# Strassen's scheme for six more output tiles of the first MLP, and two moves of single steps, in a one-core transformer kernel

## The reference, cut to what matters

```python
def _sq_relu_mlp(h, w1, w2):                     # first block, d_ff = 4096
    return jnp.square(jax.nn.relu(h @ w1)) @ w2
...
        y_x = _sq_relu_mlp(_modulate(x, g_pre_mlp[l], sh2, sc2), w_mlp_in[l], w_mlp_out[l])
        x = x + gt2 * _rmsnorm(y_x, g_post_mlp[l])
...
def mem_group(q_raw, mem_h, w_mem_kv, q_norm, k_norm):       # second block
    k = rmsnorm(kv[:, :, 0], k_norm)             # over the 128 features of each of 4 heads
...
        x = x + (mix @ w_out[l]).astype(x.dtype) # mix: latent attention, recurrence, memory attention
```

## Time and profile before

| | us |
|---|---|
| median of 3 runs | 1296.88 (1296.52 to 1297.44) |
| profiled execution | 1297.27 |
| its span from first to last instruction | 1296.0 |
| TensorE busy | 1281.8 (99%) |
| VectorE, ScalarE, GpSimd busy | 965.0, 781.6, 822.3 |
| granted TensorE clock | 1.0 in the whole span |

### The profile page before, as it was taken

One profiled execution on the slowest core, in us unless ns is written; L12 is line 12 of the kernel. 1 busy time (PEld: TensorE's weight loads), 2 busy tenths in 40 slices (PEclk: granted clock), 3 DMA queues, 4 the chain that ended last, 5 costly groups with the idle time before them and its releaser, 6 DMA issues.

```text
span 1296.0 us, 22880 instructions
## 1 busy us (share of the span) xinstructions
PE 1281.8 (99%) x8718; PEld 1138.4 (88%) x8718; DVE 965.0 (74%) x1685; ACT 781.6 (60%) x1488; POOL 822.3 (63%) x592
## 2 busy tenths in 40 slices
PE   9999999999999999999999999999999999999998
PEld 6787778879999999988788788777789999999998
DVE  5796694878778989834468575747579887987888
ACT  4532585478677585865655547735487655765664
POOL 2643434978778687656467372643378876887785
PEclk9999999999999999999999999999999999999999
DMA  9685235352333333533332112110223332333233
GB/s 378 237 322 205 84 135 208 110 186 93 124 106 100 101 103 107 179 98 101 127 112 82 44 57 74 57 66 33 66 82 103 110 99 98 103 110 115 98 104 109
DMA packets 42125, 156.35 MB, mean 121 GB/s; under 512 B 4384, under 2 KB 5152, under 8 KB 40992
## 3 DMA queue, kind: packets, MB, share of 16 engines
q1 hardware_dynamic: 41136, 151.60, 34.0%
q0 software_dynamic: 448, 2.62, 0.6%
q10 hardware_dynamic: 432, 0.67, 0.1%
HBM read 149.90 MB, written 4.19 MB: 119 GB/s over the span
## 4 chain that ended last, share of the span: by engine, by line
PE 77%; DVE 11%; ACT 5%; POOL 5%; issue 2%; DVEq 0%; ACTq 0%; POOLq 0%
PE bank L879 21%; PE bank L881 20%; PE bank L880 20%; PE bank L1437 2%; POOL wL L3794 2%; PE bank L928 1%; PE bank L930 1%; PE bank L929 1%; PE bank L982 1%; POOL acc L3804 1%; DVE small L2932 1%; POOL wL L3799 1%; PE bank L975 1%; PE bank L942 1%; PE bank L967 1%
## 5 line engine op out<-in xcount | busy, mean ns | idle before, releaser
L3794 POOL TENSOR_TENSOR wL<-raw,wH 128x1024 fp32r<-128x1024 f32 (+1 forms) x91 | 226.1, 2489 | 228.7 <-ACT wH L1805 225.6
L879 PE MATMUL bank<-hH,wH 128*128 128x512 f32 (+1 forms) x544 | 210.4, 387 | 1.6 <-POOL wL L3794 0.6
L881 PE MATMUL bank<-hH,wL 128*128 128x512 f32 (+1 forms) x544 | 200.6, 369 | 0.0
L880 PE MATMUL bank<-hL,wH 128*128 128x512 f32 (+1 forms) x544 | 200.4, 368 | 0.0
L3799 POOL TENSOR_TENSOR wL<-raw,wH 128x512 fp32r<-128x512 f32 (+1 forms) x120 | 154.6, 1289 | 31.1 <-ACT wH L1814 30.5
L879 PE MATMUL bank<-gH,wH 128*128 128x256 f32 x512 | 145.4, 284 | 0.3 <-POOL gL L3799 0.3
L881 PE MATMUL bank<-gH,wL 128*128 128x256 f32 x512 | 144.9, 283 | 0.0
L880 PE MATMUL bank<-gL,wH 128*128 128x256 f32 x512 | 144.9, 283 | 0.0
L1805 ACT ACTIVATE wH<-raw 128x1024 fp32r<-128x1024 f32 (+1 forms) x91 | 95.2, 1048 | 54.6 <-PE bank L881 28.3
L879 PEld LDWEIGHTS bank<-hH,wH 128*128 128x128 f32 x544 | 102.8, 189 | 25.3 <-issue 6.5
L881 PEld LDWEIGHTS bank<-hH,wL 128*128 128x128 f32 x544 | 102.6, 189 | 18.0
(11 more groups left out here) (537 smaller groups left out, 4087.4 us busy)
## 6 DMA issues: line engine op xcount, KB each, us to landing
raw<-in_wall SPq DMA_DIRECT2D x211, 512.0 KB, 3.3
rows<-in_wall SPq DMA_DIRECT2D x24, 1024.0 KB, 11.1
bra<-in_rpbw SPq DMA_DIRECT2D x8, 360.0 KB, 4.5
xq<-in_xt SPq DMA_DIRECT2D x2, 1024.0 KB, 6.9
xT<-in_xn SPq DMA_DIRECT2D x1, 2048.0 KB, 7.6
out_x<-xT SPq DMA_DIRECT2D x1, 2048.0 KB, 8.6
xT<-out_x SPq DMA_DIRECT2D x1, 2048.0 KB, 9.4
out_x<-xT SPq DMA_DIRECT2D x6, 256.0 KB, 2.6
```

Source lines behind the costliest of these rows:

```text
L879: matmul(o, a_h, b_h, start=first, stop=False)
L880: matmul(o, a_h, b_l, start=False, stop=False)
L881: return matmul(o, a_l, b_h, start=False, stop=last)
L3794: tt(wL[i % NHL][:, 0:n], raw[load(c) % NRAW][:, 0:n], wH[i % NHL][:, 0:n].bitcast(F32), ALU.subtract).then_inc(s.w_lo, 1)
```

## The change

Three edits.

1. **Six of the last eight output tiles by Strassen.** `FIRST_MLP` gets three more outer pairs (12, 13, 14; G grows from 26 to 29 pairs), for the output tiles 0 to 5 of the last quarter. Tiles 6 and 7 stay direct, in halves. The forms of the last four activation pairs are now made like all others, bH and bL are gone, and the late half of the tokens for tiles 6 and 7 gets buffers of its own (xlast, xlH, xlL). The residual x is read back into another buffer (xr). The four statistics move into the last pairs: mk0 after product 5 of pair 13, mk1 and mk2 after products 2 and 5 of pair 14, mk3 after the first half of tile 6. Squares and sums of y are regrouped around the last pair.
2. **The first pair's last piece.** `piece_high(0, 6)` and its `piece_rest` go ahead of the steps for the second activation form.
3. **Latent attention.** The pieces of w_out_2 before the items 2, 4, ..., 14 are cut in two: two k-tiles before the item, two behind it.

```diff
@@ plan and pairs
-        if quarter < 3:
-            for j in range(4):
-                for i, odd in ((0, 0), (1, 0), (1, 1), (0, 1)):
-                    tile("w_mlp_out", 2 * j + i, range(8 * quarter + odd, 8 * quarter + 8, 2))
-        else:
-            group([("w_mlp_out", m) for m in range(2)], OUT_ORDER)
-            for m in range(2, 8):
-                tile("w_mlp_out", m, OUT_ORDER)
+        for j in range(4 if quarter < 3 else 3):
+            for i, odd in ((0, 0), (1, 0), (1, 1), (0, 1)):
+                tile("w_mlp_out", 2 * j + i, range(8 * quarter + odd, 8 * quarter + 8, 2))
+    for m in (6, 7):
+        tile("w_mlp_out", m, OUT_ORDER)
...
-             + [("outer", 4 * quarter + j) for j in range(4 if quarter < 3 else 0)]]
+             + [("outer", 4 * quarter + j) for j in range(4 if quarter < 3 else 3)]]
@@ TensorE
+        KEY_PLACE = {(G - 2, 5): 0, (G - 1, 2): 1, (G - 1, 5): 2}
+
+        def memory_statistic(i):
+            statistic_of_halves(f"mk{i}", 256, BANK["mk", i])
...
+                if (n, q) in KEY_PLACE:
+                    memory_statistic(KEY_PLACE[n, q])
...
-        outs = [claim(BANK["w_mlp_out", m]) for m in range(2)]
-        for i, k in enumerate(OUT_ORDER):
...
-        for m in range(6):
-            b = BANK["w_mlp_out", m]
-            if m >= 2:
-                tile("w_mlp_out", m, OUT_ORDER, [(claim(b), XB)])
-            freed[b] = s.y_full, m + 1
-            if 0 < m < 5:
-                statistic_of_halves(f"mk{m - 1}", 256)
...
+                if (i, m) == (0, 6):
+                    memory_statistic(3)
@@ TensorE, latent attention
-                tile("w_out_2", i % 8, range(lo, lo + 4), [(claim(b), MM)])
-                freed[b] = s.part, i + 1
+                part_of_tile(i, range(2) if parted(d) else range(4))
...
+            if step.piece in PART and parted(step.piece):
+                part_of_tile(PART[step.piece], range(2, 4))
@@ ScalarE
         piece_high(0, 5)
+        piece_high(0, 6)
...
         odd_high(1)
-        piece_high(0, 6)
         even_high(1)
...
+            if not more:
+                memory_root(0)
+                memory_square(1)
+                first_product(n)
+                ahead("w_mlp_out", OUT_ORDER[0], 6, 2)
+                memory_root(1)
+                memory_square(2)
+                result_square(2)
+                result_square(3)
+                memory_root(2)
+                memory_square(3)
+                continue
...
         activation(lb[:, 2, :], lb[:, 2, :], ACT.Exp).then_inc(s.lb_a, 1)
...
+        ahead("w_mlp_out", OUT_ORDER[0], 6)
+        result_square(4)
+        result_square(5)
+        memory_root(3)
@@ VectorE, in the loop over the pairs
+            if outer_of(n) == 13:
+                low_sums("mk0")
+            if outer_of(n) == 14:
+                memory_key(0)
+                low_sums("mk1")
+                memory_key(1)
+                low_sums("mk2")
             product_sums(n)
...
         first_sum(G - 1)
+        added(G - 1, 2)
+        memory_key(2)
+        low_sums("mk3")
@@ GpSimd
-        for q in (0, 1, 3, 5):
+        for q in (0, 1, 3, 5, 6):
             piece_rest(0, q)
...
             if n + 1 == G:
-                ahead("w_mlp_out", 24, 0, 2)
+                ahead("w_mlp_out", OUT_ORDER[0], 6, 2)
+                result_sum(2)
+                result_sum(3)
                 continue
...
+            if outer_of(n) == 12:
+                pool.wait_ge(s.full, FULL.b + 33)
+                rest(xlL[:, :, :], xlast[:, :, :], xlH[:, :, :], s.rest_g)
...
+        ahead("w_mlp_out", OUT_ORDER[0], 6)
+        result_sum(4)
+        result_sum(5)
@@ SyncE
             if i == last_inner:
-                sp.wait_ge(s.prod, outer_done(2))
+                sp.wait_ge(s.prod, 7 * (INNER[13] + 1))
                 sp.wait_ge(s.x_moved, 32)
-                nc.sync.dma_start(xT[:, :, :], out).then_inc(s.x_moved, 16)
+                nc.sync.dma_start(xr[:, :, :], out).then_inc(s.x_moved, 16)
```

More of the change, by code:

```diff
@@ L50 @@
 GROUPS = ((0, 8), (8, 16), (16, 22))
-OUT_ORDER = [24 + i for i in (0, 1, 2, 3, 4, 5, 7, 6)]
+OUT_ORDER = range(24, 32)
+Y_ORDER = (1, 0, 3, 2, 5, 4)
 def plan_weights():
@@ L441 @@
 MULT = before(hc=8, h2=8, b=3)
-FULL = before(first=16, hm=8, h2=4, b=24, fs=22)
+FULL = before(first=16, hm=8, h2=4, b=33, fs=22)
 REST = before(first=8, hm=4, h2=8, fs=22)
-REST_G = before(first=8, hm=4, s2=4, b=24, form=4, fb=22)
+REST_G = before(first=8, hm=4, s2=4, b=33, form=4, fb=22)
 X2_S = before(x2=8, up=22)
@@ L678, in build @@
     xl = at("xl", R + 92 * K, [128, 256])
+    xlast = at("xl", 88 * K, [128, 4, 256])
+    xlH = at("xlH", R + 56 * K, [128, 4, 256], F32R)
+    xlL = at("xlL", R + 60 * K, [128, 4, 256], F32R)
+    ysum = at("ysum", R + 66 * K, [128, 512])
+    ysq = [at("ysq", R + (68 + 2 * i) * K, [128, 512]) for i in range(2)]
+    xr = at("xr", R + 72 * K, [128, 8, 512])
     sS = [at("sS", R + (24 + 4 * i) * K, [128, 1024]) for i in range(2)]
@@ L1610, in dense, with parted, part_of_tile @@
                     statistic("om", [(acc[0][:, :], 0, 128)])
-                b = BANK["part", i]
-                lo = 4 if i < 8 else 8
-                tile("w_out_2", i % 8, range(lo, lo + 4), [(claim(b), MM)])
-                freed[b] = s.part, i + 1
+                part_of_tile(i, range(2) if parted(d) else range(4))
+        def parted(d):
+            return any(t.piece == d and t.latent in (2, 4, 6, 8, 10, 12, 14) for t in STEPS)
+        def part_of_tile(i, part):
+            b = BANK["part", i]
+            lo = 4 if i < 8 else 8
+            o = claim(b) if 0 in part else bank[b]
+            tile("w_out_2", i % 8, range(lo, lo + 4), [(o, MM)], part)
+            freed[b] = s.part, i + 1
         def head_statistics(d):
@@ L3213, in added, with memory_key @@
             tt(y[:, m, :], y[:, m, :], sum_bank(n, (1, 3)[count - 1]), ALU.add).then_inc(s.y, 1)
+        def memory_key(i):
+            dve.wait_ge(s.root, rooted(f"mk{i}"))
+            dve.wait_ge(s.ones, 5)
+            stt(out=kM[:, i, :], in0=kM[:, i, :], scalar=vc("mem_k"), in1=xl[:, :], op0=ALU.mult,
+                op1=ALU.mult).then_inc(s.mk_n, 1)
         plain_squares()
@@ L3267, in vector_program @@
         tt(coef[:, 4, :], mod[:, 40:48, 0], vcs("g_post_mlp"), ALU.mult).then_inc(s.coef_c, 1)
-        low_sums("mk0")
-        for m in range(6):
-            dve.wait_ge(s.product, out_done(max(m, 1)))
-            dve.wait_ge(s.y, Y.half + 24)
-            tt(y[:, m, :], y[:, m, :], bank[BANK["w_mlp_out", m]], ALU.add).then_inc(s.y_full, 1)
-            if 0 < m < 4:
-                low_sums(f"mk{m}")
-            if 0 < m < 5:
-                dve.wait_ge(s.root, rooted(f"mk{m - 1}"))
-                dve.wait_ge(s.ones, 5)
-                stt(out=kM[:, m - 1, :], in0=kM[:, m - 1, :], scalar=vc("mem_k"), in1=rs[(m - 1) % 2][:, 0:256],
-                    op0=ALU.mult, op1=ALU.mult).then_inc(s.mk_n, 1)
         def last_tiles(i):
@@ L3948, in gpsimd_program @@
             piece_rest(n + 1, 6)
-        for m in range(8):
-            if m not in (1, 7):
-                ahead("w_mlp_out", OUT_ORDER[4 if m == 0 else 0], m)
-            if 0 < m < 6:
-                if m > 1:
-                    pool.wait_ge(s.add_g, ADD_G.f + m - 1)
-                add_squares(acc[0][:, :], m, s.sq, SQ.f)
+            if outer_of(n) == 13:
+                result_sum(1)
+        ahead("w_mlp_out", OUT_ORDER[0], 6)
+        result_sum(4)
+        result_sum(5)
         def late_squares(i):
```

176 lines of the change are left out of this document (77 added, 99 removed).

## The result

The changed kernel takes 1301.26 us (median of 6 runs, 1300.66 to 1303.06) beside 1297.16 for the kernel before (6 runs, 1296.26 to 1297.59): ratio 1.0035, 95% interval 1.0024 to 1.0046. It is 4.1 us slower; I had forecast 1294.7 and a range up to 1297.7. Its profiled execution took 1300.74, with a span of 1299.4.

A forecast was written before the change was run, and what follows sets the result against it. TensorE, busy 99% of the span, was taken to bound the kernel. Edits of +2.1, -1.7 and -2.7 gave -2.3 on 1297.27, so 1295.0; less 0.39 for the median 1294.6, taken as 1294.7 us, range 1291.0 to 1297.7.

The forecast's parts named there:

- TensorE's own work, -2.4: Edit 1: six direct tiles of 24 matmuls go, three pairs of 84 come, statistics stay four; net -2.4 us.
- mk2, 1.9: Last pair: TensorE waits 1.9 us at mk2's statistic for VectorE's low part, ScalarE having two weight chunks ahead of mk1's root.
- VectorE's low part T + 10.75: Last pair, T its start: mk2's high part ends about T + 10.3, its low part T + 10.75; TensorE comes at T + 8.87.
- I cost that at nothing: GpSimd's eighth operation in pair 12, xlL, makes it 1.1 us late; counted as no cost, pair 13's pieces having 1.2 us slack.
- My slower rival: Late half of tokens (xlH, xlL) delays pair 13's piece 3; all 3.4 us stretch pair 13, giving 1298.1; chance 0.08.
- The half statistic, 2.5: First half statistic: TensorE waits 2.5 us for GpSimd's third chunk part, two whole sums and half sum.
- mk3, 0.1: After tile 6's first half: TensorE waits 0.1 us for mk3's low part, behind VectorE's sums, adds and mk2's key.
- Edits 2 and 3, -1.7 and -2.7: First pair's idle before product 6 goes, -1.7 us; latent attention's waits for ScalarE's copy are covered, -2.7 us.
- the rival that latent attention only moves its waits: Latent attention: the next wait, exponentials or second transposition, takes over, so edit 3 gives 0 and time is 1297.4; chance 0.12.
- Edit 1's +2.1: Strassen edit in total: -2.4 of TensorE's work plus 4.5 us of three waits, between -2.4 and +4.1.

The follow-up runs named there:

- e5_quiet: The changed kernel with GpSimd holding back its second chunk's low part and the two sums until mk2's low part is made: 1300.72 us.
- e10_psum: e9_root0 with the roots of mk1 and mk2 left in their PSUM bank, so VectorE's key multiplication reads one operand from PSUM: 1293.31 us.
- e7_mk0: e4_root_first with GpSimd making xlL a pair later and ScalarE making mk0's square and root earlier: 1299.88 us.
- e9_root0: e6_half with mk0's square and root earlier on ScalarE, VectorE's mk0 low part ahead of the piece's, xlL left in pair 12: 1293.83 us.
- e11_best: e10_psum with VectorE's low parts ahead of key multiplications, mk0's ahead of the fourth weight sum, mk1's square earlier, lb steps behind adds: 1292.87 us.
- e4_root_first: The changed kernel with mk1's root and mk2's square and high part ahead of the second weight chunk on ScalarE, last pair: 1298.37 us.
- e6_half: e4_root_first with the third weight chunk ahead of the lb steps on ScalarE, and its low part behind the half sum on GpSimd: 1295.42 us.
- e8_all: e4_root_first with the further moves of e6_half and e7_mk0 together: 1296.63 us.
- e12_both: The kernel before with edits 2 and 3 alone: 1293.16 us, and 1293.17 us when run again beside e11_best.
- e3_strassen: The changed kernel without edits 2 and 3, so the Strassen edit alone: 1306.18 us.

## Why the prediction was wrong

*TensorE's own work, -2.4.* The sum stands: with the four gaps (8.32 us), the 0.5 of pair 12 (nearly all of it the wait for `pL`) and the slow clock's 1.4 taken off the 8.2 that edit 1 cost, -2.0 remains, so little else is hidden in it.

*mk2, 1.9: mis-sized, 4.14.* The step that failed is "Root, square and start of the high part are 1.25 apart ... and VectorE's low part T + 10.75". (That sentence has a slip as well: 8.75, 1.25 and 0.42 make T + 10.4, so the same count gives 2.0.) ScalarE's part came as counted. VectorE's 0.42 came from steps of the kernel before that had an idle GpSimd beside them, and the key's multiplication had no term, since at 0.48 us it is over before the high part is; here GpSimd ran through, first the chunk's low part and then the two sums that this change puts behind it, and the two steps took 1.48 and 1.87. e5_quiet gives 2.04 when that is taken away, e10_psum shows which operands matter. The trace of before had a case that I did not read: a key's multiplication of 0.87 us where the others take 0.48, beside a GpSimd sum.

```profile
591.99 0.87 DVE L3278 SCALAR_TENSOR_TENSOR kvM<-kvM,vecs,rs 128x256 f32<-128x256 f32 x1 [1.51 <-ACT rs L1826]
```

```profile
591.28 1.29 POOL L3804 TENSOR_TENSOR acc<-acc,tmp 128x512 f32<-128x512 f32 x1 [0.85 <-ACT tmp L1829]
```

*mk0: not in the sum.* I had counted from the start of the last pair on, and mk1 indeed did not wait; mk0, a pair earlier, waits 1.80 us, since its low part is behind the fourth weight sum, which waits for GpSimd, and then itself waits for GpSimd. Its root, behind a piece and two squares, holds the bank that product 1 of the last pair needs: 0.84. "I cost that at nothing", of GpSimd's load in pair 13, is the sentence: GpSimd is busy 12.05 of 12.30 us there. My slower rival had the place nearly right and the mechanism wrong: xlL itself is not what holds TensorE (e7_mk0 moves it and gains nothing; with it in its place the other moves of e9_root0 bring mk0's gap to 0.59, and e11_best's to nothing), a GpSimd that is hardly ever idle is.

*The clock, not in the sum at all.* 1.4 us behind mk2, shown by the granted clock. It went where the wait went (e4_root_first, e5_quiet) and away with the waits (e6_half). With gaps of 2.1 to 2.8 us it differs from one execution of the same kernel to the next (e7_mk0, e8_all), and these runs do not show what decides it.

*The half statistic, 2.5.* Right as a mechanism and in size where nothing shades it (2.79 and 2.76); 1.54 in the changed kernel, because TensorE itself was late.

*mk3, 0.1.* Right in the changed kernel, where TensorE was late; 0.98 to 1.11 once mk2 is mended.

*Edits 2 and 3, -1.7 and -2.7.* Right as mechanisms: 3.6 to 3.9 us together by the two comparisons, against 4.4. Edit 2 gave 1.74. Edit 3 gave 2.1, 0.6 less than forecast; the rival that latent attention only moves its waits is true for this much, with the 0.63 us in front of the scores, and this wait stands in e12_both too.

Edit 1's +2.1 became +8.2; the other two gave -3.8 of their -4.4. The error of the time is edit 1's: 2.2 us at mk2, 2.6 around mk0, 1.4 of the clock, 0.5 in pair 12 and 0.4 of its own work, less 1.0 at the half statistic and 0.1 at mk3.

## What to carry over

A VectorE step's duration holds only beside the same neighbour: ask for each one on the path whether both its tensors lie in SBUF and what GpSimd does in that microsecond. With several handoffs between TensorE and the slow engines in a stretch, the waits do not add: one hides the next, and mending one shows it. Exchanging TensorE's work for less work pays only where its statistics can be a few microseconds late.

## What the hardware showed that was not expected

- VectorE's steps with two SBUF operands waited for a running GpSimd step in full: 0.41 us became 2.59 beside one of 2.55 us, and 0.48 became 1.9 beside one of 2.4; with one operand in PSUM it was 0.48 in the same place. Where GpSimd's steps follow each other without a pause, the VectorE step came in between two of them. Behind mk0's low part the second of the two took 1.47 to 1.49 us in the changed kernel, e9_root0, e10_psum and e11_best, where its neighbours took 1.28 to 1.31.
- Even a tiny one of 128 x 4 elements with a single tensor, a TENSOR_SCALAR, took 1.28 us in e6_half beside a GpSimd sum of 1.29 us (the first of the two in the second row) and 0.17 in e4_root_first, where GpSimd was idle. A TENSOR_TENSOR of the same size with two SBUF operands took 1.25 in e10_psum beside such a sum, and 0.15 elsewhere. So neither a small size nor a single tensor kept a step from waiting:

```profile
599.48 1.28 DVE L3293 TENSOR_SCALAR lb<-lb 128x4 f32<-128x4 f32 x1
```

```profile
599.44 2.73 POOL L3935 TENSOR_TENSOR ysum<-ysum,ysq 128x512 f32<-128x512 f32 x2 [1.89 <-ACT ysq L1845]
```

- One gap of 4.1 us in a stream of matmuls was followed, 0.9 us after its end, by 3.2 us at half the clock (0.50, so 1.2 GHz instead of 2.4); in e3_strassen the same gap was followed by it at once, for more than 5 us. Gaps near 2.8 us that came behind smaller ones were followed by it too in the profiled executions of e4_root_first and e5_quiet, but not in that of e7_mk0. In e8_all, whose longest gap was 2.1 us, seven of eleven executions had a mean clock under 1.0; in e6_half, whose longest was 1.8 us, none had. A lower clock can therefore cost one execution of a kernel 1 us or more and spare the next, and a profile of one execution need not show it.
